# Two transformer blocks in fp32: the gated blocks' output product, norm and first gate and up product, token tile by token tile

## The reference

```python
for l in range(DEPTH):
    last = l == DEPTH - 1
    ...
    x = x + g1 * branch_merge(ya, yb, ga, gb, w_pa[l], w_pb[l], w_o[l])
    if not last:
        ctx = ctx + cg1 * branch_merge(ya_c, yb_c, gac, gbc, w_pa[l], w_pb[l], w_o[l])
    h2 = modulate(rms_norm(x, norm2[l]), sh2, sc2)
    x = x + g2 * swiglu_2(h2, w_ffn_in[l], w_ffn_out[l])
    if not last:
        hc2 = modulate(rms_norm(ctx, norm2[l]), csh2, csc2)
        ctx = ctx + cg2 * swiglu_2(hc2, w_ffn_in[l], w_ffn_out[l])
```

## Time and profile before

| | |
|---|---|
| median of 3 runs | 1810.4 us |
| the three runs | 1808.3, 1810.4, 1814.79 us |
| span of the profiled execution | 1814.2 us |
| busy: PE, PE weight loads | 1765.5, 1444.1 us (97%, 80%) |
| busy: POOL, DVE, ACT | 1346.3, 930.4, 899.4 us (74%, 51%, 50%) |
| HBM | 190 GB/s over the span |

### The profile page before, as it was taken

One profiled execution on the slowest core, in us unless ns is written; L12 is line 12 of the kernel. 1 busy time (PEld: TensorE's weight loads), 2 busy tenths in 40 slices (PEclk: granted clock), 3 DMA queues, 4 the chain that ended last, 5 costly groups with the idle time before them and its releaser, 6 DMA issues.

```text
span 1814.2 us, 29552 instructions
## 1 busy us (share of the span) xinstructions
PE 1765.5 (97%) x10046; PEld 1444.1 (80%) x10046; DVE 930.4 (51%) x1898; ACT 899.4 (50%) x1404; POOL 1346.3 (74%) x776
## 2 busy tenths in 40 slices
PE   9988999979999999999999999999999999999997
PEld 7767888867888897788888977788888977788886
DVE  4567665563554554455555564545456665441112
ACT  6455444566444555644445455554446445554343
POOL 7368998434988687588888874588886894678884
PEclk9999999999999999999999999999999999999999
DMA  7767786424887644357886462368774563346552
GB/s 273 193 205 243 240 270 212 143 88 156 286 264 241 212 147 156 127 181 223 261 257 225 154 185 86 113 206 269 253 248 159 170 208 99 117 151 196 186 186 69
DMA packets 268425, 347.27 MB, mean 191 GB/s; under 512 B 20264, under 2 KB 181416, under 8 KB 268328
## 3 DMA queue, kind: packets, MB, share of 16 engines
q1 hardware_dynamic: 265152, 339.40, 58.6%
q10 hardware_dynamic: 3176, 6.62, 1.2%
HBM read 342.20 MB, written 1.64 MB: 190 GB/s over the span
## 4 chain that ended last, share of the span: by engine, by line
PE 88%; DVE 6%; ACT 3%; issue 1%; DMA 1%; POOL 0%; SPq 0%; ACTq 0%; DVEq 0%; POOLq 0%
PE bank L2447 23%; PE bank L2449 23%; PE bank L2448 23%; PE bank L2586 3%; PE bank L3187 2%; PE bank L2515 1%; PE bank L2517 1%; PE bank L2516 1%; PE bank L3177 1%; PE bank L3226 1%; PE bank L2610 1%; PE bank L2570 0%; DVE X L1547 0%; ACT wh L844 0%; ACT xf L928 0%
## 5 line engine op out<-in xcount | busy, mean ns | idle before, releaser
L807 POOL TENSOR_TENSOR wl<-raw,wh 128x1024 fp32r<-128x1024 f32 x300 | 730.7, 2445 | 112.1 <-ACT wh L1009 86.9
L2447 PE MATMUL bank<-wh,xh 128*128 128x512 f32 (+1 forms) x1590 | 625.2, 393 | 9.2 <-POOL wl L795 2.5
L2449 PE MATMUL bank<-wl,xh 128*128 128x512 f32 (+1 forms) x1590 | 612.4, 385 | 0.0
L2448 PE MATMUL bank<-wh,xl 128*128 128x512 f32 (+1 forms) x1590 | 611.2, 384 | 0.0
L794 POOL TENSOR_TENSOR wl<-raw,wh 128x512 fp32r<-128x512 f32 (+1 forms) x232 | 310.0, 1336 | 323.1 <-ACT wh L844 312.6
L1009 ACT ACTIVATE wh<-raw 128x1024 fp32r<-128x1024 f32 x270 | 286.5, 1062 | 434.9 <-PE bank L2449 424.7
L2447 PEld LDWEIGHTS bank<-wh,xh 128*128 128x128 f32 x1590 | 299.6, 188 | 71.7 <-issue 5.6
L844 ACT ACTIVATE wh<-raw 128x1024 fp32r<-128x1024 f32 (+2 forms) x268 | 275.0, 1049 | 155.7 <-PE bank L2449 88.3
L2449 PEld LDWEIGHTS bank<-wl,xh 128*128 128x128 f32 x1590 | 299.3, 188 | 61.0
L2448 PEld LDWEIGHTS bank<-wh,xl 128*128 128x128 f32 x1590 | 300.0, 189 | 55.2
L795 POOL TENSOR_TENSOR wl<-raw,wh 128x512 fp32r<-128x512 f32 (+1 forms) x232 | 309.9, 1336 | 0.0
(11 more groups left out here) (414 smaller groups left out, 2030.0 us busy)
## 6 DMA issues: line engine op xcount, KB each, us to landing
raw<-in_w_ffn_in SPq DMA_DIRECT2D x264, 256.0 KB, 3.0
raw<-in_w_in SPq DMA_DIRECT2D x224, 256.0 KB, 3.0
arena<-in_w_mod SPq DMA_DIRECT2D x76, 512.0 KB, 5.2
raw<-in_w_ffn_out SPq DMA_DIRECT2D x132, 256.0 KB, 3.5
raw<-in_l_w_gate SPq DMA_DIRECT2D x88, 256.0 KB, 3.8
raw<-in_l_w_up SPq DMA_DIRECT2D x88, 256.0 KB, 4.5
raw<-in_l_w_down SPq DMA_DIRECT2D x88, 256.0 KB, 4.1
raw<-in_w_o SPq DMA_DIRECT2D x48, 256.0 KB, 2.9
```

What stands on the lines that cost most here:

```text
L807: nc.gpsimd.tensor_tensor(wl[:, s, :], raw[:, s, :], words(wh)[:, s, :], ALU.subtract)\
L2447: mm(dst, x_hi, w_hi, start=first, stop=False, skip_group_check=True)
L2448: mm(dst, x_lo, w_hi, start=False, stop=False, skip_group_check=True)
L2449: return mm(dst, x_hi, w_lo, start=False, stop=last, skip_group_check=True)
```

## The change

In the three gated blocks:

- Output tile 1 runs as two passes over its four chunks, t = 0 and then t = 1 (`tile_rows`). A chunk is counted as used in the second pass. Between the parts of the second pass PE transposes the residual: after part 0 the eight transposes of the first half for both t, after part 1 the four of the second half for t = 0, after part 2 the root of t = 0.
- The first gate and up product runs as two passes (`gate_up_rows`), t = 0 and then t = 1, chunks counted as used in the second. In the first, after chunk 2, PE transposes the second half for t = 1, after chunk 3 the root of t = 1.
- Root, scaling, shift and low part work on one row tile at a time: 128x128 instead of 128x256, and twice as many instructions. DVE's residual addition for (tile 1, t = 1) stands within the norm of t = 0 (`last_rows`).
- ACT's `gated_roots` becomes `gated_halves` and one `gated_root` a row tile, with `hi_until` calls between them. `tail(o_..)` ahead of them is as before.
- `keep_pace(8, ...)` ahead of the FFN goes, in each of the three blocks.

```diff
@@ -606,11 +610,15 @@
+        def column_half(name, k, t):
+
+            if t and k >= 4:
+                return bank[2 + k % 2][:, P * (k // 6):P * (k // 6) + P]
+            return column(name, k)[:, P * t:P * t + P]
...
@@ -1290,14 +1301,28 @@
-            def mod_norm(name, s, l, shift, meanwhile):
...
+            def mod_norm(name, s, l, shift):
+                src, g, first = (C, X)[s], SPREAD.index(name), plan.first[name]
+
+                def shifted_high(t, pairs):
+                    rows = slice(t * P, t * P + P)
+                    for k in range(2 * pairs[0], 2 * pairs[-1] + 2):
+                        act.wait_ge(norm_mid, KD * (TT * g + t) + k + 1)
+                        nc.scalar.activation(xh[:, k, rows], column_half(name, k, t), ACT.Identity, bias=mod_col(l, shift, k, s))\
+                          .then_inc(norm_xt, 1)
+
+                hi_until(first + 2)
+                gated_halves(name, src)
+                gated_root(name, src, 0)
+                hi_until(first + 3)
+                shifted_high(0, (0, 1))
+                hi_until(first + 4)
+                shifted_high(0, (2,))
+                gated_root(name, src, 1)
+                shifted_high(0, (3,))
+                hi_until(first + RING)
+                for pair in range(4):
+                    shifted_high(1, (pair,))
...
@@ -1398,8 +1423,7 @@
                 tail(f"o_{name}")
-                mod_norm(f"ffn_{name}", s, l, 3,
-                         lambda: hi_until(plan.end(f"o_{name}") + RING))
+                mod_norm(f"ffn_{name}", s, l, 3)
...
@@ -1469,39 +1493,69 @@
-            def spread_norm(name, shift):
+            def spread_norm(name, shift, last_rows):
...
+                root(0)
+                spread_root(0)
+                scaled(0, 0)
+                scaled(0, 1)
+                low(0, 0)
+                scaled(0, 2)
+                low(0, 1)
+                last_rows()
+                scaled(0, 3)
+                low(0, 2)
+                low(0, 3)
+                root(1)
+                spread_root(1)
+                scaled(1, 0)
+                scaled(1, 1)
+                low(1, 0)
+                scaled(1, 2)
+                low(1, 1)
+                low(1, 2)
+                scaled(1, 3)
+                low(1, 3)
...
@@ -2148,21 +2202,26 @@
             def gated_gemm(name, dst):
                 dve.wait_ge(gate_set, 2 * gate_no[name] + 2)
...
+                for n, t in ((0, 0), (0, 1), (1, 0)):
+                    gated_rows(name, dst, n, t)
...
@@ -2382,7 +2441,8 @@
-                spread_norm(f"ffn_{name}", lambda k: mod[:, l, k % 4, 6 + k // 4, s:s + 1])
+                spread_norm(f"ffn_{name}", lambda k: mod[:, l, k % 4, 6 + k // 4, s:s + 1],
+                            lambda: gated_rows(f"o_{name}", dst, 1, 1))
...
@@ -2495,6 +2555,23 @@
+            def tile_rows(name, i, t, after):
+
+                width, parts = plan.tiles[name][i][1:]
+                x = slice(t * P, t * P + P)
+                for part, (j, k0, rows) in enumerate(parts):
+                    chunk_ready(j)
...
+                    if t == TT - 1:
+                        ins.then_inc(chunk_used, 1)
+                    elif part == len(parts) - 1:
+                        ins.then_inc(o_rows, 1)
+                    after(part)
...
@@ -2617,8 +2689,52 @@
+            def root_row(name, t):
+
+                pe.wait_ge(norm_xn, TT * norm_no[name] + t + 1)
+                tr(bank[2][:, 2 * P:3 * P], rstd[:, t:t + 1].broadcast_to([P, P]), ident).then_inc(root_spread, 1)
...
+                def gate_up_rows(t, after):
+
+                    x = slice(t * P, t * P + P)
+                    at = split_at[name] + 4 * t
+                    for c in range(GU_CH):
...
+                            pe.wait_ge(xt_split, at + c + 1)
...
+                        if t == TT - 1:
+                            ins.then_inc(chunk_used, 1)
+                        after(c)
...
@@ -2704,11 +2820,20 @@
+                    def last_root(c):
+                        if c == 2:
+                            half_turn(name, 1, (1,))
+                        if c == 3:
+                            root_row(name, 1)
+
+                    gate_up_rows(0, last_root)
+                    gate_up_rows(1, lambda c: None)
...
@@ -3274,13 +3393,18 @@
                 pe.wait_ge(evac, plan.tile_no[f"o_{name}"] - 1)
-                for part in range(4):
-                    tile_chunk(f"o_{name}", 1, part, rows_done=o_rows if part == 3 else None)
-                rows_turn(f"ffn_{name}", (0, 1))
-                pe.wait_ge(gate_set, 2 * gate_no[f"ffn_{name}"] + 2)
-                rows_turn(f"ffn_{name}", (2, 3))
-                root_rows(f"ffn_{name}")
-                keep_pace(8, gub0[0])
+                tile_rows(f"o_{name}", 1, 0, lambda part: None)
+
+                def first_root(part):
+                    if part == 0:
+                        pe.wait_ge(gate_set, 2 * gate_no[f"ffn_{name}"] + 2)
+                        half_turn(f"ffn_{name}", 0, (0, 1))
+                    if part == 1:
+                        half_turn(f"ffn_{name}", 1, (0,))
+                    if part == 2:
+                        root_row(f"ffn_{name}", 0)
+
+                tile_rows(f"o_{name}", 1, 1, first_root)
                 ffn(f"ffn_{name}", h2, ahead={"c0": "mix_x0", "x0": "mix_c1"}.get(name))
```

More of the change, by code:

```diff
@@ L294, in build @@
     early_no = {n: i for i, n in enumerate(EARLY)}
+    xt_at, n_xt = {}, 0
+    for n in NORMS:
+        xt_at[n] = n_xt
+        n_xt += KD * (TT if n in SPREAD else 1)
     x_half_at = {n: TT * i for i, n in enumerate(RES[0:4])}
@@ L890, in gated_roots, with gated_root @@
                 step(nc.scalar.activation(sumsq4[:, 2:4], sumsq4[:, 0:2], ACT.Identity, scale=1.0 / D, bias=eps6))
-                hi_until(plan.first[name] + GU_CH + 1)
+            def gated_root(name, src, t):
+                n = norm_no[name]
+                flat = xf.rearrange("p a b -> p (a b)")
                 settle()
[L893 to L899, removed]
+                residual_done("o" + name[3:], t)
+                act.wait_ge(norm_ss, TT * n + t)
+                nc.scalar.activation(flat[:, 512:], src[:, t, 512:], ACT.Square, accum_out=sumsq[:, t:t + 1]).then_inc(norm_ss, 1)
+                act.wait_ge(norm_ss, TT * n + t + 1)
+                nc.scalar.activation(std[:, t:t + 1], sumsq[:, t:t + 1], ACT.Sqrt, scale=1.0 / D, bias=sumsq4[:, 2 + t:3 + t])\
+                  .then_inc(norm_std, 1)
             def norm_turned(name, scale, shift):
@@ new lines, in root, with spread_root, scaled @@
+                def root(t):
+                    dve.wait_ge(norm_std, TT * n + t + 1)
+                    v.reciprocal(rstd[:, t:t + 1], std[:, t:t + 1]).then_inc(norm_xn, 1)
+                def spread_root(t):
+                    dve.wait_ge(root_spread, TT * g + t + 1)
+                    step(v.tensor_copy(rdiag[:, t, :], bank[2][:, 2 * P:3 * P]))
+                    settle()
+                def scaled(t, pair):
+                    rows = slice(t * P, t * P + P)
+                    for k in (2 * pair, 2 * pair + 1):
+                        dve.wait_ge(half_col, 3 * g + (1, 2 + t)[k >= 4])
+                        v.scalar_tensor_tensor(out=column_half(name, k, t), in0=column_half(name, k, t), scalar=nscale[:, k:k + 1],
+                                               in1=rdiag[:, t, :], op0=ALU.mult, op1=ALU.mult).then_inc(norm_mid, 1)
@@ new lines, in low @@
+                def low(t, pair):
+                    rows = slice(t * P, t * P + P)
+                    for k in (2 * pair, 2 * pair + 1):
+                        dve.wait_ge(norm_xt, xt_at[name] + KD * t + k + 1)
+                        ins = v.scalar_tensor_tensor(out=xl[:, k, rows], in0=column_half(name, k, t), scalar=shift(k),
+                                                     in1=words(xh)[:, k, rows], op0=ALU.add, op1=ALU.subtract)
+                        ins.then_inc(xt_split, 1) if k % 2 else step(ins)
@@ L2496, in tile_chunk @@
                 ins.then_inc(chunk_used, 1)
+            def tile_rows(name, i, t, after):
[3 more added lines that the diff above has]
+                    chunk_ready(j)
+                    s = j % RING
+                    for r in range(rows):
+                        w, k = slice(r * width, (r + 1) * width), k0 + r
+                        ins = product(pair_of(name, i)[t][:, 0:width], xh[:, k, x], xl[:, k, x], wh[:, s, w], wl[:, s, w],
+                                      part == 0 and r == 0, part == len(parts) - 1 and r == rows - 1)
+                    if t == TT - 1:
[3 more added lines that the diff above has]
+                    after(part)
             def turned_tile(name, i, grouped):
```

109 lines of the change are left out of this document (53 added, 56 removed).

## The result

The kernel after has a median of 1829.2 us (1825.98 to 1835.54, 5 runs); beside it the kernel before had 1810.4 us (1808.3 to 1819.14, 5 runs). The ratio is 1.009, 95% interval 1.0065 to 1.0114: slower, by 16.3 us (the two medians alone are 18.8 us apart). Its profiled execution has a span of 1827.4 us.

What follows compares the result with a forecast made beforehand. It took TensorE (PE) as the bound, with 88% of the chain. Per block 5.0 us of added idle and 0.4 for the clock, 5.4; three blocks 16.2 on the 1810.4 median gave 1826.6 us, range 1819.5 to 1836.

Steps and rivals of the forecast that it cites:

- The block's sum: Each gated block: same work, new PE idle of 8.3 us against 3.3, so +5.0 us.
- ACT's chain: Ahead of root 0: conversions of FFN chunks 2 and 3 wait for the second row pass; root out at 1617.0 us.
- The first idle: PE ahead of the first root transpose, waiting for root 0: 4.5 us a block.
- The later idles: PE waits behind the first root transpose, in both gate passes: 0.43, 0.28, 1.02, 1.79 and 0.28 us.
- The three small ones: PE waits of 0.43 us behind the last output part and 0.28 us at pair 1 of each row tile.
- two such restarts: Old kernel's PE between output and gate products: two slower restarts after waits, 0.08 us each.
- Prices of the half-width forms: 128-wide scaling on DVE taken as 0.26 us apart, 0.34 long; ACT's shift as 0.37 us.
- rival 1: Half-width operations cost as much as 256-wide ones, plus full clock price: taken as 1836 us in total; chance 0.13.
- The clock: TensorE's grant falls behind the 4.5 us idle in each block: 0 to 1.3 us, taken as 0.4.
- Behind it nothing is late: FFN weights after the first gate tile arrive in time, so the loss neither shrinks nor grows there.
- Rival 2: The two conversions find their slots free, so ACT is not held: +0.5 us a block, 1811.9 us; chance 0.06.
- Rival 3: Row pass covers transposes and norm, root 0 in time: each block loses its 3.2 us, 1800.7 us; chance 0.04.

Runs made afterwards that it cites:

- e2_filler: After, with 38 matmuls of unused result put ahead of the first root transpose in each gated block; 1830.5 us, ratio 1.0084.
- e1_no_tail: After, without ScalarE's tail call for the output product ahead of the norm of each gated block; 1816.6 us, ratio 1.0005.
- e4_reordered: e1_no_tail with both root transposes, the second-half turns and VectorE's second root moved earlier; 1805.8 us, ratio 0.9953 to before.
- e5_row_passes: Before, with only output tile 1 run in two row passes, slots freed in the second; 1824.0 us, ratio 1.0048.
- e3_no_filler: Before, without its 16 idle matmuls a block; 1817.9 us, ratio 1.0017.

## Why the prediction was right, step by step

- **The block's sum, +5.0 us at full clock: measured 5.0** (e2_filler, 37.64 to 37.67 less 32.6).
- **ACT's chain.** Root 0 was put at 14.98 us into the stretch (1617.0 - 1602.02) and came at 15.05; its transpose was put at 15.44 and came at 15.38. The two conversions were to come some 4 us later than in before, each started by a product of the second row pass, the table load behind them: so it is, 7.19 and 9.44 us into the stretch instead of 3.10 and 5.82. e1_no_tail shows that this is the cause.
- **The first idle, 4.5 us: the profile shows 4.20.** Half of the difference is a matter of counting. I counted from the moment when PE could start the next instruction, 0.23 us after the start of a product; the profile counts a product as busy to its modelled end, 0.39 us, so each wait behind a product shows 0.16 us smaller. By my count it is 4.36.
- **The later idles.** By the same count (six products in 1.45 us, a transpose 0.11) e1_no_tail has 1.69 ahead of the second gate tile (1.79 predicted) and 0.93 at pair 2 (1.02). The three small ones (0.43, 0.28, 0.28) come out at 0.32, 0.21 and 0.21. With the first one that is 7.7 us where I had 8.3, so the idle terms were 0.6 too large together.
- **A term left out.** The measured 5.0 leaves 0.6 for it (5.0 + 3.3 - 7.7). Behind a wait the second product starts 0.31 us after the first (1636.85 to 1637.16) instead of 0.23. I set two such restarts against the old kernel and none against the new, which has five waits that end with a product (counted in e1_no_tail): some 0.4 us. The switches between transposes and products cost nothing more: from the first of eight transposes to the second product behind them it is 1.10 us (1616.64 to 1617.74), just 0.87 and 0.23. The other 0.2 stays open; e4_reordered, which has no wait at all, is still 0.16 above before less its 3.23 us of idle and filler (29.53 against 29.37). So the sum was right because two errors of one size cancelled, and that is luck.
- **Prices of the half-width forms.** I took 0.26 us apart for DVE's scaling and 0.37 for one of ACT's shifts. Grouped by shape, after has (count: min/median/max ns):

```profile
L1513 DVE SCALAR_TENSOR_TENSOR bank<-bank,small,rdiag x48: 348/351/359, 811.4 to 1639.1; 128x128 f32<-128x128 f32 x48
L1311 ACT ACTIVATE xh<-bank,mod x48: 348/361/373, 811.8 to 1639.5; 128x128 fp32r<-128x128 f32 x48
```

  and four scalings take 1.13 us, (1.13 - 0.35) / 3 = 0.26 apart. The near end was right, the far end (rival 1) is out. The estimate from the Trainium skill, "VectorE: DVE Perf Modes", section on the TRN2 errata (0.26 us for 128 elements from PSUM), agrees with that spacing, but not with the 0.351 us that one instruction is shown to take. Its advice against many small tiles, which it gives for operations that read SBUF, did not decide here, since e4_reordered hides them all.
- **The clock, 0.4 us a block: 0.03, 0.43 and 0.76, mean 0.41.** My upper end of 1.3 does not follow from its terms (2.7 less 1.7 is 1.0). The direction of the argument held (the low stretch eats the later waits for DVE: the 0.75 us wait at pair 2 does not appear in after at all). That the mean fits is luck, the spread between blocks is as large as the term.
- **Behind it nothing is late:** the stretches between the blocks agree within 0.3 us, as shown above.
- **The rivals.** Rival 2 (+0.5 a block if ACT is not held) is what e1_no_tail measures: +0.6. Rival 3, the faster side, gave 3.2 us a block won; e4_reordered wins 3.1. Its condition, root 0 out before PE is there, is right but was not enough: in e1_no_tail it is met, and the second root chain still costs. I had put all of rival 3 on the first root.
- **The total.** 1810.4 x 1.009 is 1826.7, forecast 1826.6; the median of after itself was 1829.2, inside the range.

## What to carry to other kernels

A buffer's release is a wait in somebody's queue: when a change moves the last use of a slot, go through the in-order queue of the engine that refills it and look at what stands behind that wait, even in lines that the diff leaves alone. Cut a hand-over chain (square, root, spread, scale, shift) loose from its place by issuing it one block of independent products earlier than it is needed, and give each chain its own block; two chains in one place cost each on its own. Idle time that follows a round trip is not cured by keeping the engine busy, only by a root that is there sooner.

## What the hardware showed that I had not expected

- The granted clock fell without any long gap. (At its lower level, 1.2 GHz for 2.4, the grant reads 0.50: so from 1625.21 to 1630.46 in after, where products start 0.43 us apart instead of 0.23.) In e5_row_passes it went to its lower level in all three blocks behind waits of 0.73, 1.37 and 0.47 to 0.62 us, and in e3_no_filler behind 0.74 and 1.90 us in one block of three with the same timeline. The Trainium skill, "TensorE: Matmul & The Clock Gate", section "Why this matters for your kernels", warns of single idle gaps longer than any of these; here it fell behind several short waits. What decides is not shown: e1_no_tail waits for 0.75 and 1.53 us and keeps its grant of 1.00.
- Filler that stands on the path is charged at the lower clock too: 16 idle matmuls took 3.21 us against 1.95 us.
- The clock's price is not its length. After has a mean grant of 0.91 in both x0 and x1 and loses 0.43 and 0.76 us there, since much of the low stretch lies over waits for other engines.
